# Expert matmuls with a stationary side of 128 columns in place of 80

## What is computed

```
xs   = gather(rms_norm(x) * (1 + scale2) + shift2, idx[e])      # 80 tokens x 1024
hid  = silu(xs @ w_gate_e[e]) * (xs @ w_up_e[e])                # 80 x 2048
y    = hid @ w_down_e[e]                                        # 80 x 1024
out[idx[e]] += gate2 * gate[e] * y                              # e = 0 .. 15
```

## Time and profile before

| | us |
|---|---|
| median of three runs | 1945.41 |
| the runs | 1941.34, 1945.91, 1945.41 |
| the profiled execution, own time | 1945.45 |
| its span, first to last instruction | 1943.6 |
| matmuls of the experts, first to last start | 839.2 to 1927.7 |

### The profile page before, as it was taken

One profiled execution on the slowest core, in us unless ns is written; L12 is line 12 of the kernel. 1 busy time (PEld: TensorE's weight loads), 2 busy tenths in 40 slices (PEclk: granted clock), 3 DMA queues, 4 the chain that ended last, 5 costly groups with the idle time before them and its releaser, 6 DMA issues.

```text
span 1943.6 us, 24164 instructions
## 1 busy us (share of the span) xinstructions
PE 1822.5 (94%) x8673; PEld 1290.0 (66%) x8673; DVE 1487.4 (77%) x1419; ACT 1155.3 (59%) x1185; POOL 393.8 (20%) x209
## 2 busy tenths in 40 slices
PE   4899999999888879579999999999999999999996
PEld 2688677877777768446666666666666666666664
DVE  4589545533377766779989989998998999899895
ACT  5444333232367761257777777777777777777773
POOL 0255401100011110003023213302321330232121
PEclk8899999999889999689999999999999999999998
DMA  8333543353222222389999999999999999999993
GB/s 284 129 119 134 196 162 126 119 169 128 83 76 66 76 66 98 115 282 373 382 376 379 384 383 379 380 382 379 378 381 381 378 382 380 379 376 383 382 380 118
DMA packets 273666, 511.35 MB, mean 263 GB/s; under 512 B 12348, under 2 KB 38244, under 8 KB 273608
## 3 DMA queue, kind: packets, MB, share of 16 engines
q1 hardware_dynamic: 264808, 487.48, 69.5%
q0 software_dynamic: 8800, 23.09, 4.2%
HBM read 488.50 MB, written 22.04 MB: 263 GB/s over the span
## 4 chain that ended last, share of the span: by engine, by line
PE 82%; DVE 6%; POOL 4%; DMA 2%; ACT 2%; SPq 2%; issue 1%; DVEq 0%; ACTq 0%; POOLq 0%
PE banks L1435 25%; PE banks L1436 24%; PE banks L1437 24%; POOL qk_swp L1331 2%; PE banks L1597 2%; POOL qk_swp L1326 1%; DMA v_h<-v_scr 1%; PE banks L1454 1%; PE banks L1455 1%; DVE w_lo L883 1%; PE banks L1693 1%; PE banks L1569 1%; PE banks L1660 1%; DVE nbias L1110 1%; DVE qk_raw L977 1%
## 5 line engine op out<-in xcount | busy, mean ns | idle before, releaser
L1295 DVE TENSOR_TENSOR w_lo<-raw_x,w_hi 128x2048 fp32r<-128x2048 f32 x192 | 437.5, 2286 | 65.4 <-ACT w_hi L861 63.7
L1295 DVE TENSOR_TENSOR w_lo<-raw,w_hi 128x2048 fp32r<-128x2048 f32 x189 | 430.9, 2287 | 35.0 <-ACT w_hi L861 31.4
L861 ACT ACTIVATE w_hi<-raw 128x2048 fp32r<-128x2048 f32 x189 | 362.7, 1919 | 110.7 <-PE banks L1437 109.2
L861 ACT ACTIVATE w_hi<-raw_x 128x2048 fp32r<-128x2048 f32 x192 | 368.0, 1917 | 84.8 <-PE banks L1437 83.8
L1435 PE MATMUL banks<-w_hi,xe_hi 128*80 128x512 f32 x1024 | 405.9, 396 | 2.2 <-issue 2.2
L1436 PE MATMUL banks<-w_hi,xe_lo 128*80 128x512 f32 x1024 | 403.8, 394 | 0.0
L1437 PE MATMUL banks<-w_lo,xe_hi 128*80 128x512 f32 x1024 | 400.1, 391 | 0.0
L1411 POOL DMA_INDIRECT out<-yeg,idx_l x32 | 146.8, 4586 | 831.5 <-DVE yeg L1257 831.5
L1435 PE MATMUL banks<-w_hi,h_hi 128*128 128x512 f32 x560 | 223.4, 399 | 2.0 <-POOL h_lo L1318 1.0
L1436 PE MATMUL banks<-w_hi,h_lo 128*128 128x512 f32 x560 | 221.7, 396 | 0.0
L1437 PE MATMUL banks<-w_lo,h_hi 128*128 128x512 f32 x560 | 221.2, 395 | 0.0
(11 more groups left out here) (200 smaller groups left out, 2230.7 us busy)
## 6 DMA issues: line engine op xcount, KB each, us to landing
raw<-in_w_gate_e SPq DMA_DIRECT2D x80, 1024.0 KB, 6.7
raw_x<-in_w_down_e SPq DMA_DIRECT2D x80, 1024.0 KB, 7.0
raw<-in_w_up_e SPq DMA_DIRECT2D x64, 1024.0 KB, 6.4
raw_x<-in_w_up_e SPq DMA_DIRECT2D x64, 1024.0 KB, 6.7
raw_x<-in_w_gate_e SPq DMA_DIRECT2D x48, 1024.0 KB, 6.0
raw<-in_w_down_e SPq DMA_DIRECT2D x48, 1024.0 KB, 6.9
raw<-in_w_in SPq DMA_DIRECT2D x28, 1024.0 KB, 5.6
raw<-in_w_ada SPq DMA_DIRECT2D x24, 1024.0 KB, 6.2
```

Of the source, the lines that this page charges most:

```text
L861: nc.scalar.activation(w_hi[:, j % NSPLIT], raw_slot(slot), ACT.Copy).then_inc(hi_done, 1)
L1295: nc.vector.tensor_tensor(w_lo[:, j % NSPLIT], raw_slot(EXPERT_SLOT[j % NRAWE]), w_hi[:, j % NSPLIT], ALU.subtract).then_inc(lo_done, 1)
```

## The change

The stationary side of every expert matmul becomes 128 columns wide. The slices still begin every 80 columns, so a slice takes in its own 80 tokens and the first 48 columns of what lies behind: the next slice, or, behind the last slice, 48 columns of zeros that are new (PAD). The matmul then writes all 128 partitions of its bank. Partitions 80 to 127 hold sums that nobody reads: ACT and DVE still read partitions 0 to 79.

- xe_hi and xe_lo grow by 48 columns. hT_hi and hT_lo become [128, 4, 368]: four rows of four slices and 48 columns of zeros each.
- POOL writes the zeros once with four memsets, between the gather for expert 0 and that for expert 1, and reports pad_ready. PE waits for pad_ready once, ahead of expert 0.
- xm, which lay ahead of xe_hi, moves to a place behind xg, where x2 lay earlier.
- ACT and DVE write hT_hi and hT_lo as one run of 320 columns, the same 320 numbers as before.

```diff
@@ buffers @@
-    xm = place("xm", [P, KT * CAP])
-    xe_hi = place("xe_hi", [P, KT * CAP], F32R)
-    xe_lo = place("xe_lo", [P, KT * CAP], F32R)
-    hT_hi = place("hT_hi", [P, FE // P, CAP], F32R)
-    hT_lo = place("hT_lo", [P, FE // P, CAP], F32R)
+    xe_hi = place("xe_hi", [P, KT * CAP + PAD], F32R)
+    xe_lo = place("xe_lo", [P, KT * CAP + PAD], F32R)
+    hT_hi = place("hT_hi", [P, 4, 4 * CAP + PAD], F32R)
+    hT_lo = place("hT_lo", [P, 4, 4 * CAP + PAD], F32R)
...
+    xm = place("xm", [P, KT * CAP], offset=WORK + 4 * D)
@@ ACT, HTO_STEP @@
-                        nc.scalar.activation(hT_hi[:, 4 * fb:4 * fb + 4, :], bank(6)[:, 0:4 * CAP].rearrange("p (k c) -> p k c", k=4),
-                                             ACT.Copy).then_inc(hth_ready, 1)
+                        nc.scalar.activation(hT_hi[:, fb, 0:4 * CAP], bank(6)[:, 0:4 * CAP], ACT.Copy).then_inc(hth_ready, 1)
@@ POOL @@
             gather(0)
             pool.wait_ge(p2_emptied, N_P2)
+            for a in (xe_hi, xe_lo):
+                nc.gpsimd.memset(a[:, KT * CAP:].bitcast(F32), 0.0).then_inc(pad_ready, 1)
+            for a in (hT_hi, hT_lo):
+                nc.gpsimd.memset(a[:, :, 4 * CAP:].bitcast(F32), 0.0).then_inc(pad_ready, 1)
@@ PE, expert @@
+                if first:
+                    pe.wait_ge(pad_ready, 4)
...
-                        ps = bank(fb % 2 * 2 + which)[0:CAP, :]
+                        ps = bank(fb % 2 * 2 + which)
...
-                            c = slice(kk * CAP, (kk + 1) * CAP)
+                            c = slice(kk * CAP, kk * CAP + P)
...
-                        ps = bank(4 + half)[0:CAP, :]
+                        ps = bank(4 + half)
...
-                            last = split3(ps, hT_hi[:, f, :], hT_lo[:, f, :], w_hi[:, s, k, :], w_lo[:, s, k, :], f == 0, f == FE // P - 1)
+                            c = slice(k * CAP, k * CAP + P)
+                            last = split3(ps, hT_hi[:, q, c], hT_lo[:, q, c], w_hi[:, s, k, :], w_lo[:, s, k, :], f == 0, f == FE // P - 1)
```

More of the change, by code:

```diff
@@ L41 @@
 CAP = CAP_L + CAP_C
+PAD = P - CAP
 GRID_W = 64
@@ L492, in trunk_program @@
         lgb_ready, lge_ready, aff_ready, idx_ready, idxg_ready = sems("lgb_ready lge_ready aff_ready idx_ready idxg_ready")
-        ampx_ready, xg_in, xt_done, xm_done, xs_done = sems("ampx_ready xg_in xt_done xm_done xs_done")
+        pad_ready, ampx_ready, xg_in, xt_done, xm_done, xs_done = sems("pad_ready ampx_ready xg_in xt_done xm_done xs_done")
         xeh_done, xe_ready, sg_ready, hid_ready, ht_done, hth_ready, ht_ready = sems("xeh_done xe_ready sg_ready hid_ready ht_done hth_ready ht_ready")
@@ L1282, in expert @@
                         dve.wait_ge(hth_ready, e * 4 + (fb + 1))
-                        nc.vector.tensor_tensor(hT_lo[:, 4 * fb:4 * fb + 4, :], bank(6)[:, 0:4 * CAP].rearrange("p (k c) -> p k c", k=4),
-                                                hT_hi[:, 4 * fb:4 * fb + 4, :], ALU.subtract).then_inc(ht_ready, 1)
+                        nc.vector.tensor_tensor(hT_lo[:, fb, 0:4 * CAP], bank(6)[:, 0:4 * CAP], hT_hi[:, fb, 0:4 * CAP], ALU.subtract).then_inc(ht_ready, 1)
                     if i == YE_STEP:
```

## The result

The change made the kernel slower: 1954.91 us, median of 6 runs (1951.65 to 1957.87), against 1943.55 (1940.69 to 1948.74, 6 runs) for the kernel before. The ratio is 1.0059, with a 95% interval of 1.0045 to 1.0074. The forecast was 1935.5 us, so the size was missed by 19 us and the sign as well. The profiled execution took 1952.81 us.

The account below looks back on a forecast made before the run. PE, never pausing in the expert stage, was taken as the bound. A pitch gain of 15.4 us less 5.6 after transposes gave 9.8, so 1945.4 became 1935.6, rounded to 1935.5 us; 8-in-10 range 1930 to 1947.

Parts of the forecast that it names:

- What bounds the kernel: Expert stage, 1088.5 of 1943.6 us: PE never pauses, so its length is 4608 matmuls at their pitch plus transposes.
- the value of the pitch: Expert matmuls, 80 to 128 columns: pitch falls from 230.0 to 226.7 ns, 15.4 us gained over 4608 matmuls.
- the slower rival: Expert matmuls: some wider loads overrun the pitch; two per chunk cost 23 us, 13 us slower net, 1958.5 us; chance 9%.
- the wide row: Input projection's profile row: 128 stationary columns at 226.7 ns a matmul, taken as the pitch for the widened expert matmuls.
- the 4-column row: Profile row of matmuls with 4 stationary columns, slices every 4 columns: 230.8 ns, used as evidence against slice offsets.
- After transposes: Expert stage, 94 places where the longer load is not hidden: 0.06 us each, 5.6 us lost; lower bound 2.8.
- The transfers: Expert weight DMAs: shortfall of 0.1 to 0.3 us an expert, 2 to 5 us over the stage, costed at nothing.
- the reserve: Raw weight slot reused after 17.0 us; 4.5 of ACT and DVE work and about 7 landing leave 5.5 us.
- Memsets, waits, unread sums: Four POOL memsets before expert 0, PE's pad_ready wait and sums in unread partitions: no cost.
- The pitch is a matter of where the slices begin: Rival, expert matmuls: starts every 80 columns set the pitch, so nothing gained, 1945.4 to 1948.2 us; no-change chance 22%.
- The wider load is no longer hidden: Rival, expert matmuls: 192 ns loads overrun the pitch, at least 0.03 us each; 13 us slower, 1958.5 us; chance 9%.
- DMA takes the gain back: Rival, expert weight transfers: the queue's pace limits PE, leaving 6.5 us of gain, 1939 us; chance 12%.

Follow-up runs that it names:

- Shift64: Kernel before the change with everything behind w_lo moved by 64 bytes (h_hi to place 192, xe_hi to 64), weights staying: 1956.91 us, one run.
- mixhl: Against the kernel after: slices 128 wide every 128 columns, hi arrays at place 128 modulo 256 bytes, lo arrays at 0: 1954.82 us, one run.
- s96w128: Against the kernel after: 128-wide slices every 96 columns, alternating between places 128 and 0 modulo 256 bytes, overlapping by 32 columns: 1960.84 us, one run.
- s128w128o128: Against the kernel after: 128-wide slices every 128 columns, all at place 128 modulo 256 bytes, level with the weights: 1932.94 us, ratio 0.9951 to before.
- s128w80o128: s128w128o128 with slices loaded 80 instead of 128 columns wide: 1958.27 us, 5 runs, ratio 1.0065 to the kernel before.
- s128w128: Against the kernel after: 128-wide slices every 128 columns, no overlap, all at place 0 modulo 256 bytes: 1959.88 us, ratio 1.0079 to before.
- s128w80o64: s128w80o128 with slices at place 64 instead of 128 modulo 256 bytes, still 80 wide: 1942.55 us, one run.

## Why the prediction was wrong

**What bounds the kernel** was read rightly. In all sixteen kernels PE never pauses in the stage and the clock is at 1.00; the stage is 4608 matmuls at their pitch, plus what follows transposes. DVE's work stayed at 61.7 to 61.9 us throughout.

**The failed step is the value of the pitch.** The term was 15.4 us of gain, 226.7 in place of 230.0 ns for 4608 matmuls. Measured were 231.7 ns, a loss of 7.8 us. The prediction bounded the term by nothing and 15.4, so a loss in the pitch lay outside them, and only the slower rival had one. "I take the wide row, since it is the one with the same width, the same engine state and the same weights": true of all three, but there was a fourth thing in which that row was special, the place of h_hi, level with the weights. Shift64 takes it away and the row reads 233.3. The prediction weighed the offsets and put them aside by the 4-column row, whose "slices have other offsets and almost the same pitch". That row differs in width and in place at once, so it could not separate them. And "the 12 starts of an expert chunk are uneven where those of the input projection are even" was the sign that should have been followed: one distance of 237 and one of 226 ns at one width and one clock say that something beside the width sets the pitch. The prediction did name this as the place where it would break ("if the pitch at 80-column offsets isn't that of the input projection").

Where the 1.7 ns between 230.0 and 231.7 come from is shown only in part. By the table, the mean over the four places is nearly the same for 128 and 80 columns (230.6 and 230.7), so at steps of 80 columns width by itself would bring nothing. Against these means the kernel after is 1.1 ns worse, which goes the way of mixhl and s96w128, and the kernel before 0.7 ns better, which nothing here explains. The means are no firmer than their entries: one comes from shift64's projection, and one place has two values.

**After transposes** the mechanism was right and the size near. Forecast were 0.06 us in each of the six places. The kernel after shows 0.045 us, somewhat less, and in the even kernel s128w128o128, where it can be read without the places mixing in, an expert is 67.42 - 24 x 2.72 = 2.14 us beyond its chunks, against 67.96 - 24 x 2.76 = 1.72 before, 0.07 us in each. There the first distance after transposes is 315 ns, 275 in the kernel before, and the next six are 230, 230, 235, 228, 232 and 230 where 226.7 is steady: 25 ns in sum, the settling that the prediction could only guess at. Over 94 places the change paid 4.2 us, of 5.6 forecast; the even kernel 6.6. The sum for the change is then 7.8 + 4.2 = 12 us, against 11.5 in the stage.

**The transfers.** The forecast that they follow without making PE wait was put to its real test only in s128w128o128, where an expert asks for its weights every 67.42 us:

```profile
raw_x<-in_w_down_e SPq DMA_DIRECT2D x5, 1024.0 KB, 10.6
...
ACT w_hi L872 <- PE banks L1452: 175.9, 230, 0.9
```

The time from issue to landing has grown to 10.6 us late in the stage (1647 to 1715 us), within the 9 to 11 that the forecast gave; the kernel before has 6.8 there (1656 to 1724 us). Between 1173 and 1241 us it was 9.5, so it grows by some 0.16 us an expert, within the shortfall of 0.1 to 0.3 us that the prediction worked out from the earlier trace rows. That working took the fall from 8.0 to 7.1 us for a queue being worked off; in the kernel before the fall soon ends (6.8 at 1181 to 1249 us, 7.3 at 1724 to 1792), so its agreement is in part luck. And ACT still waits for PE. By the prediction's own count of the reserve, 17.0 - 4.5 - 10.6 = 1.9 us of it were left (an estimate).

**Memsets, waits, unread sums:** nothing, as forecast.

**The rivals.** "The pitch is a matter of where the slices begin" was right in its kind, and its price of nothing was wrong: it took for granted that another width at the same steps keeps the pitch of 230.0. "The wider load is no longer hidden" came nearest in time (1958.5 against 1954.91), but that is luck, since its mechanism is not what happened. With the same 189 ns load the pitch is 226.7 or 233.3, by the place alone, and a load of 148 ns has a pitch of 233.3 in s128w80o128. "DMA takes the gain back" fell.

Where the wide row's condition is met, the sum holds: 9.8 us of gain forecast, 1088.5 - 1080.0 = 8.5 us in the stage of s128w128o128, which is (230.0 - 226.7) x 4608 = 15.2 us for the pitch less 6.6 after transposes. Its whole time of 1932.94 us, against the 1935.5 forecast, holds the variation of the earlier stages too.

## What to carry to other kernels

Where the starts of like matmuls are uneven, find what the uneven ones differ in before taking a pitch from another part of the program, addresses included. A row may be carried over only if it agrees in the address of its operands too; where it doesn't, both ends of the range stay open, and a loss is among them. For matmuls like these (fp32r, back to back, 512 moving columns), place 128-column stationary slices at steps of 128 columns and level with the moving operand modulo 256 bytes; for 80 columns the best place tried was 128 bytes from it. Here that gave 1932.94 us at 128 columns and, without widening anything, 1937.69 at 80.

## What the runs showed of the hardware

- The pitch of these fp32r matmuls depends on the address of the stationary slice relative to the moving operand, modulo 256 bytes, and on the width: 226.7 to 233.3 ns at one clock. A shift of 64 bytes in the kernel before, which leaves every instruction in its order, cost 13 us (1956.91 in one run, against 1943.55), and moving the weights by the same 64 bytes gave it back (1943.26).
- The best and the worst place are opposite for 128 and 80 columns (226.7 and 233.3 against 233.3 and 228.3).
- In most chunks of s128w128 the distances alternate, 237 or 238 and 229 ns in turn; in s128w128o128 all are 226 or 227 in nearly all chunks without transposes. In s128w80o64 two patterns hold at one place and width, 2.77 and 2.72 us a chunk, so these two alone don't fix the pitch. The pattern changes after transposes; what chooses it isn't shown.
- Loads take 189 ns at 128 columns, 162 at 96 and 148 at 80, and this length doesn't order the pitches. "TensorE: Matmul & The Clock Gate" of the Trainium skill, in its section on the back-to-back issue gap, gives two figures for 512 moving columns: about 216 ns for the gap by the moving columns alone, and about 131 ns for a stream in which loads and matmuls set the spacing together. The traces agree with neither (226.7 to 233.3 ns).
- What stays open is the mechanism. A conflict between the reads of the stationary and the moving side would fit the dependence on their relative place, but no run shows it, and neither "the start decides" nor "the end decides" fits the table. Nor was the change itself run with its 80-column steps and other first places for all its slices. Moving operands of other widths or types were not tried.
